# Prompt attention: GpSimd scales the probabilities, transposes move them whole, one float32 product takes the place of three

## The reference

```python
# kind 0, latent attention: q and k have 96 columns a head, v has 64
s = (q_nope @ k_nope.T + q_rope @ k_rope.T) * MLA_SCALE      # causal: NEG where key > query
p = softmax(s);  o = p @ v
# kind 1, dilated windows (128, 1), (512, 4), (2048, 16): q, k, v have 64 columns
p_g, lse_g = softmax_lse(where(valid_g, q @ k.T * DIL_SCALE, NEG))
o = sum_g softmax(lse)_g * (p_g @ v)
```

## Time and profile before

| | |
|---|---|
| median of three runs | 2251.68 us (2250.58 to 2256.98) |
| span of the profiled execution | 2248.7 us; 3.0 below the median |
| prompt attention in it | 281 to 730 us |
| its pairs, from the first scores of one to those of the next | 52.7, 52.4, 53.2, 53.6, 55.7, 53.9, 55.1 us |
| busy: PE / DVE / ACT / POOL | 1950.7 / 937.4 / 760.0 / 359.0 us |

### The profile page before, as it was taken

One profiled execution on the slowest core, in us unless ns is written; L12 is line 12 of the kernel. 1 busy time (PEld: TensorE's weight loads), 2 busy tenths in 40 slices (PEclk: granted clock), 3 DMA queues, 4 the chain that ended last, 5 costly groups with the idle time before them and its releaser, 6 DMA issues. The chain is left out here.

```text
span 2248.7 us, 31470 instructions
## 1 busy us (share of the span) xinstructions
PE 1950.7 (87%) x10899; PEld 1706.7 (76%) x10899; DVE 937.4 (42%) x1823; ACT 760.0 (34%) x1482; POOL 359.0 (16%) x310
## 2 busy tenths in 40 slices
PE   3999879998887587857888499699999999999997
PEld 3888768887776477756666378688888888888885
DVE  5433246666665434313444343233333333323335
ACT  4222146566665444414544232212111211112112
POOL 0000000000000442001333100222211212122211
PEclk9999979998999666658999799799999999999999
DMA  6222175555554221028664350211011110111002
GB/s 217 92 101 99 48 244 196 196 187 187 186 186 168 80 57 46 21 50 219 165 164 122 90 180 23 90 57 48 28 38 56 54 40 28 47 56 47 20 27 83
DMA packets 137071, 227.19 MB, mean 101 GB/s; under 512 B 12351, under 2 KB 112960, under 8 KB 132352
## 3 DMA queue, kind: packets, MB, share of 16 engines
q1 hardware_dynamic: 131622, 157.31, 23.1%
q0 software_dynamic: 5376, 68.95, 9.0%
HBM read 201.14 MB, written 91.93 MB: 130 GB/s over the span
## 5 line engine op out<-in xcount | busy, mean ns | idle before, releaser
L2088 DVE TENSOR_TENSOR acc<-f_dp,acc 128x512 f32<-128x512 f32 x198 | 136.7, 691 | 195.3 <-PE f_dp L2169 195.3
L897 PE MATMUL a_t<-a_diag,a_pr 128*128 128x128 f32 x1152 | 151.4, 287 | 23.8 <-DVE a_diag L809 12.1
L897 PEld LDWEIGHTS a_t<-a_diag,a_pr 128*128 128x128 f32 x1152 | 143.3, 202 | 27.2 <-DVE a_pl L816 13.2
L2169 PE MATMUL f_dp<-f_dh,f_ah 128*128 128x512 f32 x396 | 155.3, 392 | 4.7 <-DVE f_al L2119 4.0
L2169 PE MATMUL f_dp<-f_dl,f_ah 128*128 128x512 f32 x396 | 154.6, 391 | 0.0
L2169 PE MATMUL f_dp<-f_dh,f_al 128*128 128x512 f32 x396 | 154.6, 390 | 0.0
L816 DVE TENSOR_TENSOR a_pl<-a_t,a_ph 128x512 fp32r<-128x512 f32 (+1 forms) x160 | 96.1, 634 | 135.6 <-ACT a_ph L739 135.4
L2102 DVE SCALAR_TENSOR_TENSOR f_gc<-f_gp,f_coef,f_gc 128x832 f32<-128x832 f32 x44 | 47.7, 1085 | 234.6 <-ACT f_lasts L2023 231.7
L719 ACT ACTIVATE a_pr<-a_pr,a_nm 128x256 f32<-128x256 f32 (+7 forms) x128 | 98.4, 769 | 114.7 <-DVE a_nm L794 114.1
L1438 POOL TENSOR_TENSOR w_vfl<-w_vf,w_vfh 96x2048 fp32r<-96x2048 f32 x16 | 74.8, 4688 | 280.7 <-ACT w_vfh L1457 280.5
L2040 ACT CAST f_ah<-f_sg 128x1088 fp32r<-128x1088 f32 x22 | 24.3, 1103 | 266.5 <-DVE f_sg L2117 266.5
(11 more groups left out here) (390 smaller groups left out, 4981.3 us busy)
## 6 DMA issues: line engine op xcount, KB each, us to landing
out_s_win_k<-in_state_win_k POOLq DMA_DIRECT2D x8, 4080.0 KB, 17.3
out_s_win_v<-in_state_win_v POOLq DMA_DIRECT2D x8, 4080.0 KB, 28.7
w_kf<-in_state_win_k SPq DMA_DIRECT2D x8, 1536.0 KB
w_vf<-in_state_win_v SPq DMA_DIRECT2D x8, 1536.0 KB
f_graw<-in_w_gate SPq DMA_DIRECT2D x22, 512.0 KB, 3.8
f_uraw<-in_w_up SPq DMA_DIRECT2D x22, 512.0 KB, 3.9
f_draw<-in_w_down SPq DMA_DIRECT2D x11, 1024.0 KB, 6.1
m_c<-in_cache_kv_latent SPq DMA_DIRECT2D x128, 64.0 KB, 1.8
```

The costliest lines, as they stand in the source:

```text
L897: last = nc.tensor.matmul(tp[(before[s] + u) % TB][:, i, h, :], pr[:, s % 2, h, (2 * u + i) * P:(2 * u + i + 1) * P], diag[:, s % 2, h, :] ...
L2088: nc.vector.tensor_tensor(a, dp[h][:], a, ALU.add).then_inc(S["d_add"], 1)
L2169: last = nc.tensor.matmul(dp[h][:], a[:, c, t * P:(t + 1) * P], w[:, c, h * 512:(h + 1) * 512], start=(c == 0 and j == 0), stop=(c == 1 an ...
```

## The change

The probabilities are normalized before the transpose, by GpSimd, in place: for each head `pr` times the reciprocal (`norm` in GpSimd's block). The transpose is then a plain one against the identity, and ScalarE copies its result as float32 into `a_pt`. The product with v is one float32 matmul for each block of keys, on `v` and `pt` as they are. The parts `vh`, `vl`, `ph`, `pl` and `diag` are gone with the instructions that made them, and so is VectorE's `low`; VectorE's `norm` becomes `over`, the reciprocal alone. There are two buffers for `v`. The loops over the pairs are written out. GpSimd's copies of the window state now stand at the head of its part of each pair, without a wait.

```diff
-        vn = sb("a_vn", [P, PT, 2 * HD])
+        vn = [sb(f"a_vn{i}", [P, PT, 2 * HD]) for i in range(2)]
-        vh, vl = (sb(n, [P, PT, 2 * HD], F32R) for n in ("a_vh", "a_vl"))
-        ph, pl = (sb(n, [P, PT, 2, P], F32R) for n in ("a_ph", "a_pl"))
+        pt = sb("a_pt", [P, PT, 2, P])
...
+            pairs = [At(kind, n, kind == 0 and n == 0) for kind in range(2) for n in range(PAIRS)]
+            for a, b in zip(pairs, pairs[1:] + [None]):
+                steps(a, b)
...
-                if not a.start:
-                    sp.wait_ge(S["v_lo"], a.pair)
-                sp.dma_start(vn[:], rows(v[0:SEQ])[:, :, cv]).then_inc(S["v_in"], 16)
+                if a.pair >= 2:
+
+                    sp.wait_ge(S["o_ps"], a.steps - PT)
+                sp.dma_start(vn[a.pair % 2][:], rows(v[0:SEQ])[:, :, cv]).then_inc(S[f"v_in{a.pair % 2}"], 16)
...
-            def turn(b, done):
-
-                pool.wait_ge(S["v_hi"], b + 1)
-                nc.gpsimd.tensor_tensor(vl[:], vn[:], vh[:].bitcast(F32), ALU.subtract).then_inc(S["v_lo"], 1)
-                pool.wait_ge(S["s_ps"], done)
-                rows = lambda ap, r: ap[bass.ds(b, 1)].rearrange("o s c -> (o s) c")[r, :]
+            def norm(a, s):
+
+                pool.wait_ge(S["recip"], a.steps + (s + 1))
+                w = (s + 1) * P
+                for h in range(2):
+                    p = pr[:, s % 2, h, 0:w]
+                    nc.gpsimd.tensor_scalar(p, p, rden[:, s % 2, h:h + 1], 1.0, ALU.mult, ALU.mult).then_inc(S["norm"], 1)
+
+            def steps(a, b):
                 for src, dst in (("state_win_k", "s_win_k"), ("state_win_v", "s_win_v")):
-                    pool.dma_start(rows(io[dst], slice(0, PAST - DEC_T)), rows(io[src], slice(DEC_T, PAST)))\
+                    pool.dma_start(io[dst][a.pair, 0:PAST - DEC_T, :], io[src][a.pair, DEC_T:PAST, :])\
                         .then_inc(io["moved"], 16)
-
-            turn(0, 2)
-            with pool.Fori(1, DEC_B) as b:
-
-                turn(b, b * (2 * PT) + 2)
+                for s in range(PT):
+                    norm(a, s)
...
-                    nc.scalar.copy(ph[:, 2 * u:2 * u + k], tp[(before[s] + u) % TB][:, 0:k]).then_inc(S["t_hi"], 1)
+                    nc.scalar.copy(pt[:, 2 * u:2 * u + k], tp[(before[s] + u) % TB][:, 0:k]).then_inc(S["t_hi"], 1)
...
-            def norm(a, s):
+            def over(a, s):
...
-                dve.wait_ge(S["recip"], a.steps + (s + 1))
-                for h in range(2):
-                    nc.vector.tensor_scalar(diag[:, s % 2, h, :], ident[:], rden[:, s % 2, h:h + 1], None, ALU.mult)\
-                        .then_inc(S["norm"], 1)
-
-            def low(a, s):
...
                 for s in range(PT):
-                    low(a, s)
                     if s + 1 < PT:
-                        norm(a, s + 1)
+                        over(a, s + 1)
...
-                            last = nc.tensor.matmul(tp[(before[s] + u) % TB][:, i, h, :],
-                                                    pr[:, s % 2, h, (2 * u + i) * P:(2 * u + i + 1) * P],
-                                                    diag[:, s % 2, h, :], start=True, stop=True)
+                            last = nc.tensor.transpose(tp[(before[s] + u) % TB][:, i, h, :],
+                                                       pr[:, s % 2, h, (2 * u + i) * P:(2 * u + i + 1) * P],
+                                                       ident[:])
...
-                        for i, (x, y) in enumerate(((vh, ph), (vh, pl), (vl, ph))):
-                            last = nc.tensor.matmul(op[s % 2][:], x[:, kb, :], y[:, kb], start=(kb == 0 and i == 0),
-                                                    stop=(kb == s and i == 2))
+                        last = nc.tensor.matmul(op[s % 2][:], vn[a.pair % 2][:, kb, :], pt[:, kb], start=(kb == 0),
+                                                stop=(kb == s))
```

More of the change, by code:

```diff
@@ L578, in prompt_attention @@
         rden = sb("a_rden", [P, 2, 2])
-        diag = sb("a_diag", [P, 2, 2, P])
         sp_ = [ps(f"a_s{h}", [P, SEQ]) for h in range(2)]
@@ L585, in prompt_attention @@
         S = {n: sem("a_" + n) for n in (
-            "const q_in k_in v_in s_ps neg_go tr_ps tr_hi tr_lo k_lo swap v_hi v_lo neg exp recip norm t_ps t_hi t_lo "
+            "const q_in k_in v_in0 v_in1 s_ps neg_go tr_ps tr_hi tr_lo k_lo swap v_hi v_lo neg exp recip norm t_ps t_hi t_lo "
             "o_ps o_half o_ev o_out").split()}
@@ L611, in walk @@
             prep[1](At(0, 0, True))
-            first = True
-            for kind in range(2):
-                if first:
-                    steps(At(0, 0, True), At(0, 1, False))
-                    with eng.Fori(1, PAIRS - 1) as n:
-                        steps(At(0, n, False), At(0, n + 1, False))
-                    steps(At(0, PAIRS - 1, False), At(1, 0, False))
-                    first = False
-                else:
-                    with eng.Fori(0, PAIRS - 1) as n:
-                        steps(At(1, n, False), At(1, n + 1, False))
-                    steps(At(1, PAIRS - 1, False), None)
+            pairs = [At(kind, n, kind == 0 and n == 0) for kind in range(2) for n in range(PAIRS)]
+            for a, b in zip(pairs, pairs[1:] + [None]):
+                steps(a, b)
         def shapes(kind):
@@ L705, in run @@
                                 last.then_inc(S["tr_hi"], 1)
-                    if part == 1:
-                        act.wait_ge(S["v_in"], a.pair * 16 + 16)
-                        if not a.start:
-                            act.wait_ge(S["o_ps"], a.steps)
-                        nc.scalar.copy(vh[:], vn[:]).then_inc(S["v_hi"], 1)
                 return run
@@ L797, in neg @@
                         accum_out=nm[:, s % 2, h:h + 1]).then_inc(S["neg"], 1)
-            def norm(a, s):
-                if s >= 2:
-                    dve.wait_ge(S["t_ps"], a.units + before[s - 1])
-                elif not a.start:
-                    dve.wait_ge(S["t_ps"], a.units)
+            def over(a, s):
                 dve.wait_ge(S["exp"], (a.steps + s) * 2 + 2)
                 nc.vector.reciprocal(rden[:, s % 2, :], den[:, s % 2, :]).then_inc(S["recip"], 1)
-                dve.wait_ge(S["recip"], a.steps + (s + 1))
-                for h in range(2):
-                    nc.vector.tensor_scalar(diag[:, s % 2, h, :], ident[:], rden[:, s % 2, h:h + 1], None, ALU.mult)\
-                        .then_inc(S["norm"], 1)
-            def low(a, s):
-                for u in range(units[s]):
-                    k = min(2, s + 1 - 2 * u)
-                    dve.wait_ge(S["t_hi"], a.units + (before[s] + u + 1))
-                    nc.vector.tensor_tensor(pl[:, 2 * u:2 * u + k], tp[(before[s] + u) % TB][:, 0:k],
-                                            ph[:, 2 * u:2 * u + k].bitcast(F32), ALU.subtract).then_inc(S["t_lo"], 1)
             def steps(a, b):
@@ L823, in steps @@
                 neg(a, 1)
-                norm(a, 0)
+                over(a, 0)
                 for s in range(PT):
-                    low(a, s)
                     if s + 1 < PT:
-                        norm(a, s + 1)
+                        over(a, s + 1)
                     if s + 2 < PT:
@@ L903, in value @@
                 if s == 0:
-                    pe.wait_ge(S["v_lo"], a.pair + 1)
+                    pe.wait_ge(S[f"v_in{a.pair % 2}"], a.pair // 2 * 16 + 16)
                 if s or not a.start:
```

5 lines of the change are left out of this document (3 added, 2 removed).

## The result

| | us |
|---|---|
| before, median of 4 runs | 2251.1 (2249.4 to 2257.0) |
| after, median of 4 runs | 2285.3 (2284.1 to 2289.9) |
| ratio, 95% interval | 1.0134 (1.0104 to 1.0164) |
| span of the profiled executions | 2248.7, then 2282.5: 33.8 more |

What follows compares the result with a forecast made beforehand. TensorE was taken as the first bound, with copies now delaying store and first loads. Against the span of 2248.7, -38 -18 -2 +2.4 +75 +7 +23 = +49.7 gave 2298.4, plus 3.0 to the median: 2301 us, range 2213 to 2335.

Steps and rivals of the forecast that it cites:

- transposes and product: On TensorE, 64 us go with 576 transpose instructions and the float32 product with v adds 26: net 38 us less.
- waits on `low`, start of kind 1, first turn: TensorE's waits: 18 us less behind `low`, 2 less at four kind 1 starts, 2.4 more before first turns.
- wait for the store: Early copies hold the old result's store, so ScalarE's first `out` waits 10.7 us in 7 pairs: 75 us more.
- low clock behind it: TensorE comes out of the store's wait at the low clock: 1 us a pair, 7 us more.
- start of the stage: First loads of q and k come behind the early copies: 23 us more, once, bounded by 19 and 26.
- The gain without the copies: Transposes, product, `low`, kind 1 starts and first turns, leaving out all terms of the early copies: -55.6 us.
- the high end: Each of a float32 product's two TensorE instructions passes its 256 columns twice: 0.224 us each, 0.448 a block.
- Rival 1: The store's rows pass between copy pieces and land within some 6 us; 75 + 7 fall away: 2219 us; chance 0.14.
- Rival 3: The float32 product costs 0.238 us a block, so TensorE has 60 us less work: 2265 us; chance 0.08.
- rival 6: A plain transpose is issued as two instructions, so the 64 us stay: 2335 us; chance 0.01.
- rival 4: GpSimd's scaling is the bound, above 2.9 us for 1024 columns; at 4 us about 2325 us; chance 0.06.
- Rival 5: TensorE's clock stays low after idling; at a mean of 0.75 a pair's work is 10 us longer: 2375; chance 0.05.

Runs made afterwards that it cites:

- e1: The changed kernel with GpSimd's two copies of every pair waiting again for that pair's first scores; 2174.6 us, 0.9644 of the kernel before.
- e2: The changed kernel with the copies waiting for the first scores in the first pair alone; 2262.0 us, 1.0032 of the kernel before.
- e3: The changed kernel with two buffers for a pair's result (a_ot) instead of one, copies still early; 2206.0 us, 0.9772 of the kernel before.
- e7: The kernel before with only the copies' place changed: issued early, once the next pair's q is transposed; 2346.7 us, 1.0390 of the kernel before.
- e5: The kernel before with GpSimd's scaling and plain transposes, three products with v kept, copies waiting; 2219.9 us, 0.9838 of the kernel before.
- e4: The changed kernel with each early copy cut into two of half the columns, rows of 1 KB; 2219.9 us, 0.9854 of the kernel before.
- e8: The changed kernel with the copies' wait put back and the scaling on VectorE instead of GpSimd; 2177.7 us, 0.9652 of the kernel before.
- e10: e1 with q, k, v loaded ahead of the tables, next pair's first scores between the halves of value(7), its exp before the last out; 2346.3 us.
- e11: The changed kernel with the first copy early and the second waiting for the pair's first scores; 2190.3 us, 0.9721 of the kernel before.
- e12: e10 with the copies behind the scaling of step 1, waiting until the old result's store has landed; 2177.2 us, 0.9648 of the kernel before.

## Why the prediction was right, and where its sum was off

Its own steps, in us on the span:

| step | predicted | measured |
|---|---|---|
| transposes and product | -37.7 | -48 |
| waits on `low`, start of kind 1, first turn | -17.6 | -22.6 |
| clock in `turn`, and scores | 0 | -7 |
| wait for the store | +75 | +66 |
| low clock behind it | +7 | +20 |
| start of the stage | +23 | +23 |
| sum | +49.7 | +31.4 by the terms; +31.6 in the stage, +33.8 in the span |

**The mechanism was right, and placed right.** Copies 10.6 us ahead of the first scores in pairs 1 to 3 and 11.7 in 4 to 7 (predicted 10.5 for all), the store landed 17.5 us after issue (near 18), the first transposes at 313.5 (near 313), seven waits of ScalarE of 10.1 us (10.7). e1 and e2 take the early copies away, e3 takes the wait away and leaves them, e7 adds them to the kernel before: each time the wait for the store, the late start or both come and go with them. That the 10.6 came so near is in part luck: in pair 0 the way from the last scores to the copies' issue took some 5.3 us instead of 6.1 (the scaling of both heads 2.2 instead of 3.0), and TensorE's way to the next pair's first scores some 16.0 instead of 16.6.

**The wait's size.** TensorE itself stood 66.3 us, and I had put ScalarE's 75. But the low clock costs more than 1 us a pair. Windows of the changed kernel, to the end of kind 0 and then of kind 1, against those of e1:

```profile
322.44:543.10 220.66, 180.88 (x976) 158.12 (x976) 75.78 (x196) 126.09 (x308) 51.04 (x72) 0.86 0.53 176
543.10:759.50 216.40, 158.84 (x816) 135.98 (x816) 73.98 (x196) 126.31 (x308) 50.11 (x70) 0.83 0.52 170
```

```profile
300.80:481.26 180.46, 169.32 (x976) 150.11 (x976) 75.75 (x196) 125.55 (x308) 51.38 (x72) 0.95 0.72 238
481.26:649.30 168.04, 149.74 (x816) 129.84 (x816) 73.80 (x196) 125.85 (x308) 51.14 (x72) 0.91 0.72 240
```

The same 1792 matmuls keep TensorE busy for 339.7 us at a mean clock of 0.86 and 0.83, and for 319.1 at 0.95 and 0.91: 20.6 us more busy time, which the lower clock takes, 3 us for each wait. The step that was too small is "4 instructions took 1.22 us ... 1 us a pair": it priced the first instructions behind an idle stretch, and the granted clock stays low for longer. In pair 1 of the changed kernel TensorE all but stands until 386.4, then works for 5.6 us at the level of 1.2 GHz before it has 2.4 again:

```profile
378.00:386.40 8.40, 0.73 (x2) 0.11 (x1) 1.17 (x4) 0.30 (x2) 0.00 (x0) 0.70 0.73 251
386.40:392.00 5.60, 4.63 (x15) 3.90 (x16) 0.17 (x1) 3.60 (x10) 1.36 (x2) 0.50 0.93 267
392.00:400.00 8.00, 8.00 (x50) 7.14 (x50) 3.76 (x9) 5.38 (x13) 1.58 (x2) 0.99 0.01 2
```

The two errors, -9 and +13, nearly cancel.

**The gain without the copies** is the larger miss: -55.6 predicted, -77.5 measured from the first scores to the last product. Here are the windows of the kernel before over both kinds; those of e1 stand above:

```profile
299.70:511.60 211.90, 195.25 (x1409) 184.40 (x1409) 133.00 (x340) 129.58 (x312) 13.74 (x13) 0.95 0.60 203
511.60:725.70 214.10, 178.75 (x1248) 165.69 (x1248) 131.99 (x340) 130.51 (x312) 13.15 (x12) 0.91 0.56 188
```

Idle time falls from 52.0 to 29.4 us, by 22.6. Busy time falls by 54.9. The count explains 48 of that, if whole groups are read from start to start. TensorE's timeline of e1, the end of pair 0:

```profile
336.34 3.19 PE L881 MATMUL a_o<-a_pt,a_vn 128*128 128x256 f32 x14
339.36 2.06 PE L867 MATMUL a_t<-a_ident,a_pr 128*128 128x128 f32 x16
341.26 1.91 PE L825 MATMUL a_s<-a_ident,a_kn 128*96 128x128 f32 x16
```

and of the kernel before, the same place:

```profile
341.63 0.36 PE L912 MATMUL a_o<-a_ph,a_vh 128*128 128x256 f32 x1
...
344.23 3.74 PE L897 MATMUL a_t<-a_diag,a_pr 128*128 128x128 f32 x32
347.80 1.91 PE L855 MATMUL a_s<-a_ident,a_kn 128*96 128x128 f32 x16
```

`value(6)` takes 3.02 us for 7 blocks, 0.431 a block (I had 0.448), and took 2.60, 0.371 (I had 0.357, leaving out the slower first product of a group): 0.060 x 288 = 17 us more, not 26. The float32 product is two instructions of 0.216 us where a float32r one of as many columns takes 0.12, so the high end was the right one; the 128/0.107 behind my 0.224 is in no row, and a line through my own two rows, 0.066 and 0.110, would have given 0.198.

`turn(7)` takes 1.90 us where it took 3.57, 0.104 less for each instruction that is gone. But it is the step that saves least. `turn(4)` of pair 0, with the first scores behind it, before and in e1:

```profile
321.61 2.40 PE L897 MATMUL a_t<-a_diag,a_pr 128*128 128x128 f32 x20
323.76 0.47 PE L883 MATMUL a_s<-a_kh,a_qh 96*128 96x512 f32 x1
```

```profile
320.54 1.25 PE L867 MATMUL a_t<-a_ident,a_pr 128*128 128x128 f32 x10
321.55 0.48 PE L853 MATMUL a_s<-a_kh,a_qh 96*128 96x512 f32 x1
```

It goes from 2.15 us to 1.01, 0.114 less for each of 10. Steps 2 to 6 save 0.114 to 0.119, and all steps together some 65 us (I had 64).

Some 7 us of busy time are left. Summed over the groups of both kinds, each from its start to the next one's with the idle time taken off, `turn` went from 135.6 to 65.7 us, `value` from 108.7 to 125.4, `scores` from 108.7 to 106.9, and the transposes of q and k from 25.1 to 24.7. Of the 70 us of `turn`, 65 are its count. The other 5 are the clock: its groups stood 17.0 us at the low level before and 7.4 in e1, and 9.6 us less at half the clock are 4.8 (an estimate). The rest is `scores`.

So of the 22 us that I missed 9 are the product's price, 6 `turn` with its clock, 2 `scores`, and 5 the waits. For the waits, the step "I take 18, since `high` can be late itself" was too small: all 22.2 us behind L816 went, and the first `turn` waits 12.9 us for the scaling in e1 where it waited 12.1 for `diag` (I had 2.4 more). The miss is in both kinds. Kind 0 went from 211.9 to 180.5 us, kind 1 from 214.1 to 168.0; my terms, with the 4.7 and 17.5 us behind L816 that the waits of before show in the two kinds, come to some 21 and 34, against 31 and 46. And e5 shows that removing `low` is worth more than its waits of before once `turn` is short: there TensorE waits 62 us for `low` and for scalings that are late behind it.

**The rivals.** Rival 1, a store that isn't held, is out for pieces of 64 KB, and nearly true for rows of 1 KB (e4: landed in 8.5 us, 3.8 us of waits in all). Rival 3 and rival 6 fall by the spacings, rival 4 by 1.125 us for 1024 columns (I took 1.5) and by e8. Rival 5, a clock that stays low, was about half there: 0.84 over the pairs, between the 0.94 of before and its 0.75.

**The page.** The store's rows didn't pass in one turn: it needed 17.5 us in the change and 26.1 in e10, and the records of both traces (under e11) show 16 rows to 16 pieces of 64 KB, which on 16 DMA engines is one row to a piece. The Trainium skill, "DMA: Bandwidth & Descriptors", section "Queues, rings and completion order", says that an engine switches between rings by whole packets of typically 9 to 17 descriptors. By that rule all 8 rows of the store on an engine would have passed at once, and the seven waits would have been gone as in e3. No run here agrees with it beside 64 KB pieces.

## What to carry to other kernels

A large DMA that nobody waits for still has a place in the order. If it is made of large pieces (64 KB here), a small transfer of several rows that is issued behind it, on another queue too, lands about when it is through, and the engine that waits for the small one pays; with short rows the hold was 8.5 us instead of 17.5 (e4). So when a wait is taken from in front of such a copy, or any edit shifts what stands around it, look at which small transfers now fall behind it, and order the copy behind their landing with a wait of its own (e12), not by the luck of 0.3 us (e1, e10). And measure the halves of a change together too: halves that gained 36 and 19 us alone gained 79 as one.

## What the runs showed of the hardware that I had not expected

- The store's landing is set by the copies' issue, not by its own. Issued 2.1 to 3.8 us behind them (e10) it took 26.1 us, 11.1 to 11.6 behind (the change) 17.5, 12.0 to 14.2 behind (e7) 16.1: each time 28.7 to 30.2 us after the copies' issue, which is when they are through. Issued 0.3 us ahead of them (e1): 3.3. With one copy ahead and one 0.3 us behind (e11) it landed in 5.9, just behind the first.
- Beside pieces of 64 KB the store's rows pass one to a piece; in the gap between the two copies two to an engine passed in e10, where it was short, and all of them in e11. The first row of a store behind the copies starts 4.5 to 5.3 us after the issue in the change, 0.9 in e1; why it starts so late stays open.
- The issuing queues are held too. In pair 1, SyncE's issue of the k load behind the store takes 12.46 us in the change and 1.02 in e1, where that of the v load then takes 25.29:

```profile
369.98 12.46 SPq L637 DMA_DIRECT2D a_kn<-scratch_s_k  x1
```

- GpSimd's issue of copies in short rows can stand for 9 to 23 us, with its arithmetic behind it (e4).
- GpSimd's scaling didn't slow VectorE beside it: `neg` over 1024 columns took 1.219 us before and 1.222 to 1.224 in the change.
